# Splitting weight tiles on ScalarE and VectorE instead of GpSimd in a hybrid encoder block

## The reference

```
h   = rms_norm(x, g_mix);  p = h @ w_in          # 8 column groups of w_in
att = sliding-window attention (8 heads of 64, 2 KV heads, ALiBi, sinks)
mh  = sigmoid(mo) * mLSTM(silu(conv(mq, mk)), mv, gates)   # 4 heads
mix = concat(rms_norm(att, g_attn_out), rms_norm(mh, g_mlstm_out))
x   = x + mix @ w_out
h2  = rms_norm(x, g_ffn)
x   = x + (silu(h2 @ w_gate) * (h2 @ w_up)) @ w_down
```

## Time and profile before

| what | value |
|---|---|
| median of 3 runs | 1141.17 us |
| span of the profiled execution | 1137.2 us |
| TensorE busy | 1114.9 us (98%) |
| VectorE busy | 420.9 us (37%) |
| ScalarE busy | 292.2 us (26%) |
| GpSimd busy | 382.7 us (34%) |
| mean granted TensorE clock | 0.992 |

### The profile page before, as it was taken

One profiled execution on the slowest core, in us unless ns is written; L12 is line 12 of the kernel. 1 busy time (PEld: TensorE's weight loads), 2 busy tenths in 40 slices (PEclk: granted clock), 3 DMA queues, 4 the chain that ended last, 5 costly groups with the idle time before them and its releaser, 6 DMA issues.

```text
span 1137.2 us, 14184 instructions
## 1 busy us (share of the span) xinstructions
PE 1114.9 (98%) x5366; PEld 915.2 (80%) x5366; DVE 420.9 (37%) x667; ACT 292.2 (26%) x651; POOL 382.7 (34%) x344
## 2 busy tenths in 40 slices
PE   9996999999999999999999999999999999999998
PEld 7894777778878888888888888888888888888886
DVE  4275348757853641130413223141312214131224
ACT  6421123347731532211121211111121111112010
POOL 3279666715673212511221221222122122212010
PEclk9997999999999999999999999999999999999999
DMA  8112211130121101311111121111112111111003
GB/s 248 37 38 73 75 38 56 47 130 30 42 89 45 39 28 37 102 47 37 53 58 37 37 70 40 37 55 55 37 42 68 37 37 55 55 37 49 25 18 148
DMA packets 70075, 65.14 MB, mean 57 GB/s; under 512 B 5272, under 2 KB 52632, under 8 KB 70040
## 3 DMA queue, kind: packets, MB, share of 16 engines
q1 hardware_dynamic: 69048, 64.18, 18.1%
q10 hardware_dynamic: 992, 0.49, 0.2%
HBM read 59.96 MB, written 4.21 MB: 56 GB/s over the span
## 4 chain that ended last, share of the span: by engine, by line
PE 89%; POOL 4%; DVE 3%; ACT 2%; issue 1%; DMA 1%; SPq 0%; DVEq 0%
PE bank L595 28%; PE bank L597 28%; PE bank L596 28%; ACT prob L1146 2%; POOL w_lo L522 1%; POOL w_raw L520 1%; POOL w_hi L518 1%; PE bank L613 1%; PE bank L682 1%; PE bank L679 1%; DVE prob L1498 1%; DVE smx L1503 1%; DMA w_raw<-in_w_in 1%; PE bank L745 0%; PE bank L658 0%
## 5 line engine op out<-in xcount | busy, mean ns | idle before, releaser
L579 POOL TENSOR_TENSOR w_lo<-w_raw,w_hi 128x512 fp32r<-128x512 f32 x132 | 169.8, 1296 | 577.9 <-ACT w_hi L984 577.4
L595 PE MATMUL bank<-actT_hi,w_hi 128*128 128x512 f32 x704 | 274.3, 390 | 0.0
L597 PE MATMUL bank<-actT_hi,w_lo 128*128 128x512 f32 x704 | 274.1, 389 | 0.0
L596 PE MATMUL bank<-actT_lo,w_hi 128*128 128x512 f32 x704 | 274.0, 389 | 0.0
L595 PE MATMUL bank<-w_hi,actT_hi 128*128 128x512 f32 (+1 forms) x448 | 174.5, 390 | 11.2 <-POOL w_lo L522 10.4
L1561 DVE TENSOR_TENSOR prod<-bank,silu 128x512 f32<-128x512 f32 x44 | 30.4, 692 | 391.9 <-PE bank L597 369.7
L597 PE MATMUL bank<-w_hi,actT_lo 128*128 128x512 f32 (+1 forms) x448 | 169.9, 379 | 0.0
L596 PE MATMUL bank<-w_lo,actT_hi 128*128 128x512 f32 (+1 forms) x448 | 169.6, 378 | 0.0
L1576 DVE TENSOR_TENSOR x<-bank,x 128x512 f32<-128x512 f32 x176 | 121.7, 692 | 122.6 <-PE bank L597 122.6
L595 PEld LDWEIGHTS bank<-actT_hi,w_hi 128*128 128x128 f32 x704 | 132.2, 188 | 27.6 <-DVE x L1467 0.3
L597 PEld LDWEIGHTS bank<-actT_hi,w_lo 128*128 128x128 f32 x704 | 132.2, 188 | 27.4
(11 more groups left out here) (179 smaller groups left out, 967.9 us busy)
## 6 DMA issues: line engine op xcount, KB each, us to landing
w_raw<-in_w_gate SPq DMA_DIRECT2D x44, 256.0 KB, 2.9
w_raw<-in_w_up SPq DMA_DIRECT2D x44, 256.0 KB, 2.9
w_raw<-in_w_down SPq DMA_DIRECT2D x44, 256.0 KB, 2.6
w_raw<-in_w_in SPq DMA_DIRECT2D x32, 256.0 KB, 3.5
w_raw<-in_w_out SPq DMA_DIRECT2D x16, 256.0 KB, 2.6
x<-in_x SPq DMA_DIRECT2D x8, 512.0 KB, 6.1
out<-x SPq DMA_DIRECT2D x16, 256.0 KB, 2.0
x_in<-in_x SPq DMA_DIRECT2D x7, 512.0 KB, 5.0
```

The costliest lines, as they stand in the source:

```text
L579: nc.gpsimd.tensor_tensor(w_lo[:, ring, :], w_raw[:, m % RAW, :], w_hi[:, ring, :].bitcast(F32), ALU.subtract).then_inc(w_ready, 1)
L595: nc.tensor.matmul(ps, x_hi, wh, start=first, stop=False)
L596: nc.tensor.matmul(ps, x_hi, wl, start=False, stop=False)
L597: return nc.tensor.matmul(ps, x_lo, wh, start=False, stop=last)
```

## The change

GpSimd's `split` and its calls go, with the semaphore `w_gained` and GpSimd's waits for units. ScalarE gets `w_high(n)`: one activation (copy with the gain as scale) from the raw tile to the high part. VectorE gets `w_low(n)`: one scalar_tensor_tensor, gain times raw tile minus high part. Both are called once per step, tile n = U for U below 48: on ScalarE after the evacuation (and, in units 0 to 5, after the next row block's high part and statistics), on VectorE before everything else of the step but the evacuation of the transposed query and key columns and the low parts of input rows.

```
+    SPLIT = 6 * K
...
         def _(pool):
-            def split(ring, raw, width, n, gain):
-                pool.wait_ge(raw_s[raw], raw_count(n))
-                w = w_raw[:, raw, 0:width]
-                g = gain.to_broadcast([P, width])
-                nc.gpsimd.tensor_tensor(w_hi[:, ring, 0:width], w, g, ALU.mult).then_inc(w_hi_s, 1)
-                pool.wait_ge(w_hi_s, n + 1)
-                nc.gpsimd.tensor_tensor(w, w, g, ALU.mult).then_inc(w_gained, 1)
-                pool.wait_ge(w_gained, n + 1)
-                nc.gpsimd.tensor_tensor(w_lo[:, ring, 0:width], w, w_hi[:, ring, 0:width].bitcast(F32),
-                                        ALU.subtract).then_inc(w_ready, 1)
...
-            pool.wait_ge(mix_ready, 1)
             for n in range(NS):
                 g = 1 + n // K
-                if g >= 2 and n % K == 0:
-                    pool.wait_ge(unit_done, (g - 1) * T)
-                c = (G_OUT if g >= 5 else G_MIX) + n % K
-                if n == 4 * K:
-                    pool.wait_ge(cols_ready, 1)
-                split((g * K + n % K) % RING, n % RAW, NKV if g == 1 else N, n, cols[:, c:c + 1])
                 if g == 4:
                     exponents(n % K)
...
+            def w_high(n):
+                act.wait_ge(raw_s[n % RAW], raw_count(n))
+                g, k = 1 + n // K, n % K
+                width = NKV if g == 1 else N
+                c = (G_OUT if g >= 5 else G_MIX) + k
+                if n == 4 * K:
+                    act.wait_ge(cols_ready, 1)
+                nc.scalar.activation(w_hi[:, (g * K + k) % RING, 0:width], w_raw[:, n % RAW, 0:width], ACT.Copy,
+                                     scale=cols[:, c:c + 1]).then_inc(w_hi_s, 1)
...
                     stats(U + 2)
+                if U < SPLIT:
+                    w_high(U)
...
+            def w_low(n):
+                dve.wait_ge(w_hi_s, n + 1)
+                g, k = 1 + n // K, n % K
+                width = NKV if g == 1 else N
+                c = (G_OUT if g >= 5 else G_MIX) + k
+                r = (g * K + k) % RING
+                V_.scalar_tensor_tensor(w_lo[:, r, 0:width], w_raw[:, n % RAW, 0:width], cols[:, c:c + 1],
+                                        w_hi[:, r, 0:width].bitcast(F32), ALU.mult,
+                                        ALU.subtract).then_inc(w_ready, 1)
...
                     low_part(U + 2, h_hi, h_split)
+                if U < SPLIT:
+                    w_low(U)
```

More of the change, by code:

```diff
@@ L256, in hymba_block @@
         w0_ready = sem("w0_ready")
-        w_gained = sem("w_gained")
         f_hi_s = sem("ffn_w_hi_done")
```

## The result

The changed kernel takes 1143.39 us (median of 11 runs, 1141.58 to 1144.78) against 1140.99 us of the kernel before on the same chips (11 runs, 1138.11 to 1142.42): ratio 1.0022, 95% interval 1.0013 to 1.0031. That is 2.4 us slower: little, but the whole interval lies above 1. The profiled execution has a span of 1140.1 us, 2.9 us more than before, and a granted clock of 0.994; it took 1141.9 us and so is one of the faster of the 11.

What follows compares the result with a forecast made beforehand. TensorE was taken as busy almost all the span, so only its idle time could be won. Terms -7.1 - 0.5 + 1.3 + 3.5 + 2.4 + 0.8 = +0.4 gave span 1137.6, time 1141.6 us; 8-in-10 range 1136.0 to 1147.0.

Steps and rivals of the forecast that it cites:

- the softmax loop: Units 35 to 41: high and low part lengthen the ring of ScalarE and VectorE; 2.4 us lost over six steps.
- Convolutions, -7.1: Units 9 to 16: convolutions without GpSimd beside them run faster, slice k=7 starts at 96.3 instead of 103.42; 7.1 us gained.
- The slow spell after the waits: Unit 16, low clock behind TensorE's waits: assumed to stay; 1.5 us more gained if the clock stayed up.
- the rival that rests on it: Convolutions don't get faster: 1.95 us is VectorE's own, k=7 comes at 109; 1154.7 us, chance 0.04.
- Gate chain, -0.5: Unit 18: two VectorE passes before the log forget gate shrink from 2.18 to 1.3 us; 0.5 us gained (0 to 0.9).
- Unit 32 to 33, +1.3: Low part 32 stands before VectorE's last mLSTM step, so the queries come late for TensorE; 1.3 us lost (0.5 to 1.7).
- Bias load, +3.5: Unit 34: ALiBi bias loads issued only after low part 34, delaying VectorE and TensorE's transposes; 3.5 us lost (2.7 to 4.5).
- clock, +0.8: Behind the last probability wait (326.16), grown to about 2.4 us: slow spell of 1.5 us, half taken; 0.8 us lost.
- ring pays in full: Rival, units 35 to 41: 0.9 us lost a step with nothing back, plus slow clock; 1145.3 us, chance 0.17.

Runs made afterwards that it cites:

- taking the gate away: Changed kernel with the two late bias loads one tile earlier in SP's order, behind low part 33 instead of 34: 1139.53 us, ratio 0.9990.
- the kernel that waits for the bias first: Changed kernel in which SP issues the four loads of x only when the two bias loads have landed: 1143.08 us, ratio 1.0021.
- with the early bias: Changed kernel with bias loads one tile earlier and, from tile 32 on, high part before the exponentials, low part before the wait for them: 1130.91 us, ratio 0.9919.
- with GpSimd doing them: Changed kernel with tiles 0 to 31 split by ScalarE and VectorE, but tiles 32 to 47 by GpSimd as before: 1132.36 us, ratio 0.9924.

## Why the prediction was right, and where its sizes were off

The forecast was +0.4 us against the span, and +2.9 came. The mechanisms of the parts were seen, with one exception (the softmax loop). That the total came so near is partly luck: attention lost 3.7 us more than forecast behind unit 34 (1.9 at the bias, 1.8 in loop and clock), and 0.9 us more than forecast up to unit 18 stands against it.

- *Convolutions, -7.1.* Right in mechanism and size: passes of 1.28 us, k=7 at 96.93 against the 96.3 worked out. The start of k=7 gained 6.5 us and not 7.1, because this whole execution was 0.6 us late from unit 0 on (unit 16 began at 86.78, 86.15 before), which isn't the change's. The slow spell after the waits, which I let stand, ended earlier and gave the 1.5 us that I had as a bound: 0.7 inside unit 16, 0.8 in unit 17. Up to unit 18 that is -8.0 us. The 1.5 us are luck of this execution: five of seven other traces of this code have the slow spell later and longer. One bound in this part doesn't follow from its rows. I took 7.9 us for a convolution whose 1.95 us were its own, but with the single-operand pass of 0.71 it is 6.6, k=7 would come near 104.5, and the rival that rests on it would be about 1150 and not 1154.7 us.
- *Gate chain, -0.5.* -0.6 between units 18 and 19.
- *Unit 32 to 33, +1.3.* The wait is 1.30 us, and +1.5 us stand between the marks of units 32 and 34.
- *Bias load, +3.5.* The gate is as told. The load is the mis-sized term: I took the 2.7 us of a raw tile from the last issue, 3.1 in all and 3.4 with some queueing; it took 5.2 in the profiled execution and 3.8 to 3.9 in four other kernels. Between unit 34 and the first prob transposes 5.4 us were lost in that trace, 1.3 us less with a load of 3.9; taking the gate away gave 3.6 us back. I named the wrong victim too: not the prob transposes, whose wait fell to 0.80 us, but the query transposes one step earlier (4.51 us), because the normalised queries stand behind the bias additions on VectorE. The delay is the same one, paid earlier.
- *Softmax loop, +2.4, and clock, +0.8.* Together +5.0 in the trace. The step of the prediction that failed is "from the end of one round to the next ... only the 0.12 us to 283.84 are slack": those 0.12 us are ScalarE's wait for TensorE, and the length of the steps was set by another ring, the one through TensorE. The low part of the mLSTM rows stands behind the high and low part, TensorE waits for it ahead of its unit, and the next evacuation, high part and low part stand behind that unit. This second ring summed to 10.28 us before, as long as the steps then (10.30 and 10.32), so it had no slack; with the high and low part it is 11.13, so 0.85 of the 1.42 us are paid in such a step, where I had 0.3 to 0.5. The 0.4 us that I booked back for small operations beside GpSimd's sum of squares didn't come (0.52 us again at 300.35), since that sum moves with TensorE and so with the ring. And I had each low part at 0.68 us: in the three steps where it runs beside GpSimd's normalisation it is 1.53. The 5.0 us lie between the forecast's 3.2 for ring and clock and the 6.9 of the rival "ring pays in full", which named the same wrong ring.
- *Clock.* I expected the slow spell behind the last prob transposes, with a chance of half. It came earlier, behind the new wait of 1.46 us at 309.55 (0.83, and 0.83 again in the kernel that waits for the bias first), and not behind the 2.00 us at 329.12 (1.00 in 330 to 340); the window after:

```profile
310.00:320.00 10.00, 10.00 (x63) 8.00 (x62) 7.66 (x14) 5.38 (x22) 2.75 (x3) 0.83 0.55 191
```

The Trainium skill ("SBUF — State Buffer", section "Who interferes with whom") says that a VectorE instruction with two SBUF inputs contends with a GpSimd instruction that reads SBUF, that the shared pair of ports is an exclusive lock, and that one-input forms contend in their two-port modes alone. The runs agree in which instructions are slowed: the passes with two inputs go from 1.28 to 2.2 us and the one-input pass over 1024 elements, 0.75 us alone, to 1.77 (which fits such a mode; no trace shows the mode), while beside GpSimd's sum of squares an 8-element addition of two inputs takes 0.52 us and the one-input one behind it 0.17. The lock isn't complete in these rows: before the change a VectorE pass of 1.28 us and a GpSimd product of 1.04 us, each beside the other, take 1.95 and 2.02 us, less than the 2.32 of both in turn. The rule would also have warned that a low part can be lengthened, though not by how much. The half throughput that I cited for the low part's form doesn't show: 0.74 us with GpSimd idle, against 0.69 us for two inputs without the scalar.

## What to carry to other kernels

An instruction put into a full pipeline costs its place, not its length: the same 0.7 + 0.7 us a step cost 7 us in all at the head of the steps and nothing that shows in the gap ahead of the next wait (with the early bias ratio 0.9919, against 0.9924 with GpSimd doing them). When you look for the ring that an added instruction lengthens, follow every consumer of what stands behind it, not only the ring that is tightest now, and sum each candidate from rows. And when work leaves one engine, look which loads are issued on the semaphore it raised: they are late by as much as the new owner is.

## What the hardware showed beyond that

- VectorE and GpSimd slow each other in both directions: three passes of 1024 elements 6.67 us instead of 3.92, GpSimd's product 1.70 us (up to 2.15) instead of 1.29, a 128x512 low part 1.77 instead of 0.75.
- The same pair of 256 KB loads took 3.8 to 3.9 us from issue to use in four kernels and 5.2 in one execution of a fifth; by the run times 5.2 us isn't the rule there either.
- The granted clock behind the same waits differs between kernels with the same code at that place: a slow spell of TensorE behind unit 16 costs between nothing and 1.6 us from the mark of unit 16 to that of unit 17 (5.45 to 7.06 us in eight traces).
